# Sliding-window attention laid among its projection panels, a norm taken by columns, eight activation slots

## The reference, cut to what matters

```python
def sliding_window_sink_attention(h, w_in, sinks, w_out):
    q, k, v = split_qkv(h, w_in)          # 16 query heads, 4 key/value heads of 64
    s = jnp.einsum('bnqhgd,bnkhd->bnhgqk', qb, kw) * (HEAD_DIM_2 ** -0.5)
    s = s - slopes[:, :, None, None] * dist
    s = jnp.where(mask[None, :, None, None], s, -jnp.inf)      # this block of 128 and the one before
    m = jnp.maximum(jnp.max(s, axis=-1, keepdims=True), sink)
    p = jnp.exp(s - m)
    denom = jnp.sum(p, axis=-1, keepdims=True) + jnp.exp(sink - m)
    o = jnp.einsum('bnhgqk,bnkhd->bqnhgd', p / denom, vw)
    return o.reshape(B, T, ATTN_Q_DIM) @ w_out
```

## Time and profile before

| what | value |
|---|---|
| median of 3 runs | 2536.35 us (2536.2 to 2538.89) |
| the profiled execution's own time | 2536.2 us |
| its span | 2534.4 us |
| busy PE / DVE / ACT / POOL | 2441.7 / 1682.5 / 928.1 / 740.1 us |
| mean granted TensorE clock | 0.987 of full speed |
| matmuls | 12016 |

### The profile page before, as it was taken

The page is one execution under the profiler, slowest core; times in us unless marked ns, Lnnn a source line. Parts: engine busy times, 40 slices in busy tenths (PEclk is TensorE's granted clock), DMA queues, the critical chain, the costliest instruction groups (busy, mean ns, idle before and its releaser), DMA issues.

```text
span 2534.4 us, 35089 instructions
## 1 busy us (share of the span) xinstructions
PE 2441.7 (96%) x12016; PEld 2072.3 (82%) x12016; DVE 1682.5 (66%) x3142; ACT 928.1 (37%) x1319; POOL 740.1 (29%) x646
## 2 busy tenths in 40 slices
PE   6999999898999999999999999999999979999998
PEld 4877878686887888888888899999999756788886
DVE  4887769688566667677642478888887685444434
ACT  4223853523233333333333333333333464222222
POOL 0000000000006666676676257777641000000000
PEclk8999999999999999999999999999999999999999
DMA  6222913254234444444456689999997202222321
GB/s 257 100 73 93 350 34 129 95 190 159 100 111 139 139 148 141 150 138 149 139 171 193 206 295 366 365 366 362 360 363 258 76 25 67 91 99 91 100 99 58
DMA packets 177221, 433.59 MB, mean 171 GB/s; under 512 B 32752, under 2 KB 81904, under 8 KB 176752
## 3 DMA queue, kind: packets, MB, share of 16 engines
q1 hardware_dynamic: 123888, 331.61, 37.8%
q0 software_dynamic: 34816, 67.41, 7.7%
q10 hardware_dynamic: 18432, 33.56, 3.6%
HBM read 371.48 MB, written 61.01 MB: 171 GB/s over the span
## 4 chain that ended last, share of the span: by engine, by line
PE 87%; DVE 9%; ACT 2%; issue 1%; DMA 1%; SPq 0%; ACTq 0%; DVEq 0%
PE ps L466 17%; PE ps L467 17%; PE ps L468 17%; PE ps L802 9%; PE ps L803 9%; PE ps L801 9%; PE ps L712 2%; DVE wlo L1398 1%; DVE ar L1451 1%; PE ps L696 1%; PE ps L704 1%; PE ps L781 1%; DVE ar L1513 1%; ACT whi L936 1%; DVE rstd L1412 1%
## 5 line engine op out<-in xcount | busy, mean ns | idle before, releaser
L1398 DVE TENSOR_TENSOR wlo<-raw,whi 128x1024 fp32r<-128x1024 f32 x426 | 521.4, 1224 | 569.7 <-ACT whi L936 568.2
L2239 POOL DMA_INDIRECT w_scratch<-ar x384 | 418.8, 1091 | 953.5 <-DVE wlo L1398 854.3
L936 ACT ACTIVATE whi<-raw 128x1024 fp32r<-128x1024 f32 x424 | 448.9, 1059 | 660.0 <-PE ps L803 403.4
L466 PE MATMUL ps<-b_hi,whi 128*128 128x512 f32 x1328 | 519.6, 391 | 3.2 <-DVE wlo L1398 3.0
L468 PE MATMUL ps<-b_hi,wlo 128*128 128x512 f32 x1328 | 517.6, 390 | 0.0
L467 PE MATMUL ps<-b_lo,whi 128*128 128x512 f32 x1328 | 517.3, 390 | 0.0
L801 PE MATMUL ps<-a_hi,whi 128*128 128x384 f32 x1024 | 342.7, 335 | 0.0
L803 PE MATMUL ps<-a_hi,wlo 128*128 128x384 f32 x1024 | 342.1, 334 | 0.0
L802 PE MATMUL ps<-a_lo,whi 128*128 128x384 f32 x1024 | 342.1, 334 | 0.0
L466 PE MATMUL ps<-a_hi,whi 128*128 128x512 f32 x816 | 326.9, 401 | 8.9 <-DVE wlo L1398 7.2
L467 PE MATMUL ps<-a_lo,whi 128*128 128x512 f32 x816 | 319.6, 392 | 0.0
(11 more groups left out here) (265 smaller groups left out, 2988.7 us busy)
## 6 DMA issues: line engine op xcount, KB each, us to landing
raw<-panels SPq DMA_DIRECT2D x430, 512.0 KB, 3.4
gelu_scratch<-ar ACTq DMA_DIRECT2D x128, 256.0 KB, 2.1
w_scratch<-rstd SPq DMA_DIRECT2D x32, 768.0 KB, 10.9
ar<-w_scratch SPq DMA_DIRECT2D x128, 192.0 KB, 4.7
ar<-gelu_scratch SPq DMA_DIRECT2D x128, 192.0 KB, 5.6
...
```

The lines of the kernel that those rows point to most:

```text
L466: pe.matmul(bank, w_h, hi[:, k, :], start=(k == 0), stop=False)
L936: act.activation(whi[:, u % SPLIT, :], raw[:, u % RAW, :], ACT.Copy).then_inc(hi_ready, 1)
L1398: dve.tensor_tensor(wlo[:, u % SPLIT, :], raw[:, u % RAW, :], f32(whi[:, u % SPLIT, :]), ALU.subtract).then_inc(lo_ready, 1)
L2239: nc.gpsimd.indirect_dma_start(experts, bass.IndirectOffsetOnAxis(offs[:, k:k + 1], 0), vals[:, k:k + 1], None)\
```

## The change: what it does

- SP loads the attention's 12 panels in another order (`SW_ORDER`): key 0, value 0, queries 0 to 3, key 1, value 1, queries 4 to 7. From the seventh on all but one use bank 3 (`SWB`), and each waits until its predecessor is drained.
- The pairs go by key tile and, within it, from block 3 down to block 0. Scores, turns and value products of pairs 0 to 2 (and the scores and turns of pair 3) stand between panels 6 to 11; the rest follows. `out_half` runs the two first SO panels in halves among the last turns. The orders on PE, ACT and DVE are written out anew. SO panels use banks 4 to 7.
- One tiny DVE instruction less in `swa_bias`.
- The query norm: the sum of squares is taken as four columns (128 x 4), root and reciprocal are of 128 x 4, four matmuls spread the result into bank 5, and `norm_apply` reads it from PSUM.
- One of the folds moves from the WO panels to the CO panels (5 and 5 instead of 4 and 6), the loads and sums of their columns move with them; the sum that came after the norm comes after WO panel 6.
- Gelu's tiles use eight slots, four in `sq` and `nt`; its loop on ACT is written out.
- Semaphores of several table loads are merged.

```diff
-SWB = (0, 2, 3, 1)
+SWB = (0, 2, 3, 1, 0, 2, 3, 3, 3, 3, 3, 3)
+SW_ORDER = (0, 2, 4, 5, 6, 7, 1, 3, 8, 9, 10, 11)
...
-ge_slot = area(A_GE, 4, T)
+ge_four = area(A_GE, 4, T)
+ge_slot = [ge_four[:, s, :] for s in range(4)] + [sq[:, s, :] for s in range(2)] + [nt[:, s, :] for s in range(2)]
...
+def values_bank(m):
+    return 2 if m < 3 else 2 + m % 2
...
-    pair_at = {3: 2, 4: 3, 8: 4, 9: 5, 11: 6, 12: 7, 13: 8, 14: 9, 19: 10, 20: 11, 21: 12, 22: 13, 23: 14, 24: 15}
+    pair_at = {3: 2, 4: 3, 8: 4, 9: 5, 11: 6, 12: 7, 13: 8, 14: 9, 16: 10, 18: 11, 19: 12, 20: 13, 21: 14, 22: 15}
...
+    for n, w in enumerate(SW_ORDER):
+        sp.wait_ge(lo_ready, SW + n - RAW + 1 - U)
+        sp.dma_start(raw[:, (SW + n) % RAW, :], panels[SW + w]).then_inc(landed[(SW + n) % RAW], 16)
...
-        if k in (3, 5):
-            mod2_sums((k + 5) // 2)
-    norm_total(2, rstd[:, :])
+        if k in (1, 4, 6):
+            mod2_sums({1: 4, 4: 5, 6: 6}[k])
+    pe.wait_ge(sq_used, 3 * KT - 1)
+    for t in range(TT):
+        pe.matmul(ps[:, 4, t:t + 1], rstd[:, t * P:(t + 1) * P], ones[:, 0:1], start=(t == 0), stop=False)
+    pe.wait_ge(sq_ready, 3 * KT)
+    for t in range(TT):
+        last = pe.matmul(ps[:, 4, t:t + 1], sq[:, (KT - 1) % 2, t * P:(t + 1) * P], ones[:, 0:1], start=False, stop=(t == TT - 1))
+    last.then_inc(sq_used, 1)
+    pe.wait_ge(rstd_ready, 3)
+    for t in range(TT):
+        last = pe.matmul(ps[:, 5, t * P:(t + 1) * P], root_col[:, t:t + 1].to_broadcast([P, P]), ident, start=True, stop=True)
+    last.then_inc(root_out, 1)
     pe.wait_ge(mod_done, 4)
-    mod2_sums(6)
...
-    for u in range(4):
-        first = u == 0
-        panel(SW + u, u, ps[:, SWB[u], :], a_hi, a_lo, r_of(SW) + u + 1, (h_ready, 3 * KT) if first else None,
+    def swa_panel(p):
+        first = p == 0
+        panel(SW + p, p % 4, ps[:, SWB[p], :], a_hi, a_lo, r_of(SW) + (p + 1 if p < 7 else p + 4), (h_ready, 3 * KT) if first else None,
               (lambda k: norm_stat(3, k, bank=1)) if first else None)
-        if u == 2:
-            pe.wait_ge(rt_ready, 4)
-    for u in range(2):
+    def turn_v(u, bank):
         pe.wait_ge(v2_feat, u + 1)
         for s in range(TT):
-            last = pe.transpose(ps[:, 4 + u, s * P:(s + 1) * P], v2_feat_sb[:, u, s * P:(s + 1) * P], ident)
+            last = pe.transpose(ps[:, bank, s * P:(s + 1) * P], v2_feat_sb[:, u, s * P:(s + 1) * P], ident)
         last.then_inc(v2_turned, 1)
-    groups = [(b, kt, half) for b in range(TT) for kt in range(2) for half in range(2)]
+    groups = [(b, kt, half) for kt in range(2) for b in reversed(range(TT)) for half in range(2)]
...
+        if m == 0:
+            pe.wait_ge(v2_done, 2)
+        elif m < 3:
+            pe.wait_ge(o2, m)
+        else:
             pe.wait_ge(o2, m - 1)
+        if m == 3:
+            pe.wait_ge(bank_free, r_of(SW) + 16)
...
+    def out_half(u, half):
+        if half == 0:
+            pe.wait_ge(lo_ready, SO + u + (1 - U))
+            pe.wait_ge(bank_free, r_of(SO) + u + 1)
+            pe.wait_ge(bias2, 4 * len(groups))
+            pe.wait_ge(o2, TT)
+        else:
+            pe.wait_ge(o2, 2 * TT)
+        for k in range(4 * half, 4 * half + 4):
+            last = split3(ps[:, 4 + u, :], u, k, b_hi[:, k, :], b_lo[:, k, :], k == 0, k == KT - 1)
+        if half:
+            last.then_inc(used, 1)
+    swa_panel(0)
+    swa_panel(1)
+    swa_panel(2)
+    turn_v(0, 4)
+    pe.wait_ge(rt_ready, 4)
+    swa_panel(3)
+    swa_panel(4)
+    norm_total(4, rstd1, bank=6)
+    swa_panel(5)
+    swa_panel(6)
+    pe.wait_ge(v2_done, 1)
+    pe.wait_ge(rt_ready, 5)
+    pe.wait_ge(bank_free, r_of(SW) + 10)
+    swa_scores(0)
+    swa_panel(7)
     swa_scores(1)
-    for m in range(len(groups) // 2):
-        if m + 2 < len(groups) // 2:
-            swa_scores(m + 2)
-        swa_turn(2 * m)
-        if m:
-            swa_values(m - 1)
-        swa_turn(2 * m + 1)
-    swa_values(len(groups) // 2 - 1)
-    def last_outputs(k):
-        if k == KT // 2 - 1:
-            pe.wait_ge(o2, len(groups) // 2)
-    pe.wait_ge(o2, len(groups) // 2 - 1)
-    strips(SO, KT, b_hi, b_lo, each=last_outputs)
+    swa_panel(8)
+    swa_turn(0)
+    turn_v(1, 2)
+    swa_scores(2)
+    swa_turn(1)
+    swa_panel(9)
+    swa_values(0)
+    swa_turn(2)
+    swa_scores(3)
+    swa_turn(3)
+    swa_panel(10)
+    swa_turn(4)
+    swa_values(1)
+    swa_turn(5)
+    swa_panel(11)
+    swa_turn(6)
+    pe.wait_ge(bank_free, r_of(SW) + 16)
+    swa_scores(4)
+    swa_values(2)
+    swa_turn(7)
+    swa_scores(5)
+    swa_values(3)
+    swa_turn(8)
+    swa_scores(6)
+    swa_turn(9)
+    swa_scores(7)
+    swa_turn(10)
+    swa_values(4)
+    swa_turn(11)
+    swa_turn(12)
+    swa_values(5)
+    out_half(0, 0)
+    swa_turn(13)
+    swa_turn(14)
+    swa_values(6)
+    out_half(1, 0)
+    swa_turn(15)
+    swa_values(7)
+    out_half(0, 1)
+    out_half(1, 1)
+    for k in range(2, KT):
+        panel(SO + k, k % 4, ps[:, 4 + k % 4, :], b_hi, b_lo, r_of(SO) + k + 1)
...
-    norm_root(2, rstd[:, :])
+    act.wait_ge(sq_used, 3 * KT)
+    act.activation(root_col, ps[:, 4, 0:TT], ACT.Sqrt, bias=EPS, scale=1.0 / D).then_inc(rt_ready, 1)
...
+        n = i * 4 + u
+        if n >= 8:
+            act.wait_ge(ge_out[n % 8], n // 8 * 16)
+        act.activation(ge_slot[n % 8], ps[:, u, :], ACT.Gelu).then_inc(bank_free, 1)
         act.wait_ge(bank_free, i * 4 + (4 + r_of(EU) + u + 1))
-        act.dma_start(ge_d[bass.ds(i * 4 + u, 1)].rearrange("a p n -> (a p) n"), ge_slot[:, u, :]).then_inc(ge_out[u], 16)
+        act.dma_start(ge_d[n], ge_slot[n % 8]).then_inc(ge_out[n % 8], 16)
...
-    with act.Fori(-(-first // 4), NK // 4 - 1) as i:
-        for u in range(4):
-            gelu(i, u)
...
+    for n in range(4):
+        bias_tiles(n)
+        swa_panel_hi(6 + n)
+    bias_tiles(4)
     swa_exp(0)
     swa_exp(1)
-    for m in range(len(groups) // 2):
-        more = 2 * m + 2 < len(groups)
-        swa_out(2 * m)
-        if more:
-            swa_exp(2 * m + 2)
-        if m:
-            swa_hi(m - 1)
-        swa_out(2 * m + 1)
-        if more:
-            swa_exp(2 * m + 3)
-    swa_hi(len(groups) // 2 - 1)
+    swa_panel_hi(10)
+    swa_exp(2)
+    swa_exp(3)
+    swa_out(0)
+    swa_panel_hi(11)
+    swa_out(1)
+    swa_exp(4)
+    swa_exp(5)
+    swa_hi(0)
+    swa_out(2)
+    swa_panel_hi(12)
+    swa_out(3)
+    swa_exp(6)
+    swa_exp(7)
+    bias_tiles(5)
+    swa_out(4)
+    swa_hi(1)
+    swa_out(5)
+    bias_tiles(6)
+    bias_tiles(7)
+    swa_out(6)
+    swa_hi(2)
+    swa_out(7)
+    swa_exp(8)
+    swa_hi(3)
+    swa_exp(9)
+    swa_out(8)
+    swa_exp(10)
+    swa_out(9)
+    swa_exp(11)
+    swa_out(10)
+    swa_exp(12)
+    swa_hi(4)
+    hi_next(0, SO, 0)
+    swa_out(11)
+    swa_exp(13)
+    swa_exp(14)
+    swa_out(12)
+    swa_hi(5)
+    swa_exp(15)
+    swa_out(13)
+    swa_out(14)
+    swa_hi(6)
+    swa_out(15)
+    swa_hi(7)
...
-        if k < 4:
+        if k < 5:
...
-        if k < 6:
-            fold_half(4 + k // 2, k % 2)
+        if k < 5:
+            fold_half(4 + (k + 1) // 2, (k + 1) % 2)
...
-    norm_rstd(2)
-    norm_apply(2, x, lambda k: gs2[:, k:k + 1], lambda k: mod[:, 3 * KT + k, 0:1], b_hi, b_lo, middle=lambda: lo(WQ + 1, 1))
+    norm_rstd(2, root_col)
+    dve.wait_ge(root_out, 1)
+    norm_apply(2, x, lambda k: gs2[:, k:k + 1], lambda k: mod[:, 3 * KT + k, 0:1], b_hi, b_lo, r=ps[:, 5, :], middle=lambda: lo(WQ + 1, 1))
...
+    def key2(kt, p):
+        dve.wait_ge(used, SW + p + 1)
+        dve.tensor_tensor(k2[:, kt, :], ps[:, SWB[p], :], rstd[:, :], ALU.mult).then_inc(bank_free, 1)
+    def value2(u, p):
+        dve.wait_ge(used, SW + p + 1)
+        dve.tensor_tensor(v2_feat_sb[:, u, :], ps[:, SWB[p], :], rstd[:, :], ALU.mult).then_inc(v2_feat, 1)
+        dve.wait_ge(v2_feat, u + 1)
+        dve.sem_inc(bank_free, 1)
...
-        dve.tensor_tensor(tiny[:, o:o + 4], tiny[:, o:o + 4], col("sinks", h, 4), ALU.max).then_inc(mx2, 1)
-        dve.wait_ge(mx2, n + 1)
-        dve.tensor_scalar(tiny[:, o + 4:o + 8], tiny[:, o:o + 4], -1.0, None, ALU.mult).then_inc(nmx2, 1)
-        dve.tensor_tensor(tiny[:, o + 12:o + 16], col("sinks", h, 4), tiny[:, o:o + 4], ALU.subtract).then_inc(nmx2, 1)
+        dve.scalar_tensor_tensor(tiny[:, o + 4:o + 8], tiny[:, o:o + 4], -1.0, less_sinks[:, h:h + 4], ALU.mult, ALU.min).then_inc(nmx2, 1)
+        dve.wait_ge(nmx2, 2 * n + 1)
+        dve.tensor_tensor(tiny[:, o + 12:o + 16], col("sinks", h, 4), tiny[:, o + 4:o + 8], ALU.add).then_inc(nmx2, 1)
...
+    query2(2, 4)
+    dve.tensor_scalar(less_sinks[:, :], col("sinks", 0, NH2), -1.0, None, ALU.mult).then_inc(mx2, 1)
+    swa_panel_lo(6)
+    norm_rstd(4, rstd1)
+    query2(3, 5)
+    swa_panel_lo(7)
+    residual(0, 4)
+    key2(1, 6)
+    swa_panel_lo(8)
+    dve.wait_ge(mx2, 1)
+    dve.wait_ge(bias_ready, NH2 // 2)
+    pair_bias(0)
+    value2(1, 7)
+    swa_panel_lo(9)
+    pair_bias(1)
```

(33 more changed lines are left out.)

143 lines of the change are left out of this document (58 added, 85 removed).

## The result

The changed kernel takes **2549.1 us** in the median of 6 runs (2544.3 to 2552.9), against 2536.3 before on the same chip: ratio 1.0044, 95% interval 1.0032 to 1.0057. It is slower by 12.8 us, where 3.75 were forecast. The profiled execution took 2550.5 us, 14.3 more than the one before.

A forecast was written before the change was run, and what follows sets the result against it. Attention was taken as bound by DVE and the chain through three engines, with PE at two thirds. Stage +6.7, norm -3.4 and folds +0.45 gave +3.75 on 2536.2: 2540.0 us, range 2523 to 2548.

The forecast's parts named there:

- The stage's waits: Attention stage: PE's waits 28.1 us instead of 21.9, more among the panels and fewer behind the last, +6.2 us.
- Rival (a): Attention stage: the 9.5 us of new waits among the panels are not met and the clock stays up, 2526.0; chance 0.22.
- The stage's clock: Attention stage: lower clock behind the waits of 4.3 and 5.1 us costs 2.2 each, 4.4 against 4.7 before, -0.3 us.
- 0.8 for restarts: Attention stage: about five more panels follow an attention product, each starting with a slower first matmul, +0.8 us.
- rival (b): Attention stage: clock stays or falls low behind turns 8 and 12 (+4) and at panel 9 (+1.8), 2545.8; chance 0.25.
- nothing was slow behind a wait of 1.23: Attention stage, kernel before: full-speed work behind waits like that at 2082.66, cited against the slower-clock case.
- low spells that go on as from 2045.56: Attention stage: upper bound, 4 us more, as second scores 7 us later were slow again in the kernel before.
- The query norm: From the last x tile to the first scaled tile: 3.4 us instead of 6.8, -3.4, bounds -4.0 and -2.2.
- Reading the scale from PSUM: Query norm's scaling: costs nothing, priced at 0.74 us against 0.76; by the skill's page some 0.5 us more.
- The moved folds: CO and WO panels: CO+7 split 1.4 us late, sums behind WO+1 wait until 574.0; +0.45 us in all.
- six panels and two more sums end at 609.1: WO panels behind the sums that wait for the moved fold: PE done at 609.1, x tile 7 at 609.3.
- Gelu's slots: Expert layer's Gelu on ACT: all 128 groups waited for PE, none for a DMA, so nothing to win, 0.

The follow-up runs named there:

- the control: The changed kernel itself, measured again on another chip: 2597.0 us against 2595.2 for the kernel before, ratio 1.0011 (0.9990 to 1.0032), stage 204.3 us.
- kept_busy: Changed kernel with 14 extra unread products in each of PE's waits ahead of turns 8 and 12: 2581.6 us, ratio 1.0017 to the kernel before.
- outs_first: Changed kernel with five of ACT's copies out moved up among the panels: 2573.8 us, ratio 0.9985 to the kernel before, stage 190.5 us.
- order_norm: Kernel before with the changed attention in a further order on PE, ACT and DVE, norm by columns, eight Gelu slots, old folds: 2567.5 us, ratio 0.9874.

## Why the prediction was wrong, step by step

The forecast was 2540.0 with most of its chance within 0.2% of the old time, and the result is 2549.1: slower, outside that band and 1 us over the range. Its mechanism was right and one kind of term was mis-sized, three times: what the lower clock costs behind a wait of PE, in the attention stage, in the norm and behind the moved fold.

**The stage's waits: right.** The layout had 2.4 ahead of turn 1, 2.1 ahead of values 0 and turn 4, 1.5 and 2.1 at turns 3 and 5, then 4.3, 2.4 and 5.1. Measured were 2.94, 2.12 and 2.21, in the control 2.95, 2.12 and 2.21, then 4.3, 2.1 and 4.0; in the control and in `kept_busy`, where the clock stayed up among the panels, also those at turns 3 and 5, 1.5 and 2.0. Rival (a), that these waits would not be met, was wrong: they are met, and `outs_first` shows they came from the ACT order that the prediction named. Together they were forecast at 28.1 us and measured at 26.9 in the control and 23.6 in the first trace.

**The stage's clock: the step that failed.** The prediction took "2.2 each, 4.4, against 4.7 before: -0.3", on the ground that two waits of over 4 us have a slow stretch behind them. With its 0.8 for restarts that makes 5.2 us of clock and restarts; by the table the stage has 14.6 in its traced execution and 10.1 in the control. In the first trace 4.5 of this surplus of 9.4 came back as shorter waits, which leaves 4.9 over what was forecast. Where it was too low: the spells behind turns 8 and 12 alone cost 5.3 (`kept_busy`), a third stands behind the 2 us wait of scores 7, and among the panels the control has one more, of 1.7 us, and the first trace three, of 3.0 and twice 1.7. That last mechanism was rival (b), with 0.25; it put 5.8 us more on the stage, where 5.3 were measured, and its 2545.8 with the folds' 4.2 make 2550.0. The evidence against it, that nothing was slow behind a wait of 1.23, did not bear on waits of 2 to 3 us. The kernel before shows more, and it was not looked for. At the EU panel of 816 a wait of 2.07 was followed by a clock of 0.58. And inside the attention the second slow scores, at 2052, were read as "low spells that go on as from 2045.56"; timeline and windows show the clock up again between the two and a second fall beside a wait of only 1.42:

```profile
2052.57 0.80 PE L852 MATMUL ps<-ar 64*128 64x256 f32 x2 [1.42 <-DVE tiny L2076]
```

```profile
2049.00:2052.00 3.00, 1.37 (x10) 0.84 (x8) 2.72 (x16) 2.22 (x11) 0.00 (x0) 1.00 0.00 0
2052.00:2056.00 4.00, 3.43 (x16) 2.54 (x16) 2.88 (x13) 2.13 (x11) 0.00 (x0) 0.57 0.01 2
```

**The query norm: -3.4 forecast, -2.3 in the traced execution.** Its working holds at full clock. In the control the step from x tile 7 to the first scaled tile takes 4.24 us, and the sum gave 0.75 for the tile and 3.4. At a lower clock it takes 5.3 (changed) or 6.4 (norm alone), since eight column products take up to 1.87 us instead of 1.05, and the spreading took 2.08 where 0.9 to 1.5 was the bound. And the old form gains from a busy PE as well: with the moved folds its wide products take 1.13 instead of 2.08 and the step 6.6 instead of 7.6. So with the same folds the norm by columns is worth 1.2 (norm alone) to 1.9 us (`order_norm`) with the old ones and 1.1 to 2.4 with the moved ones, by how much of it the clock slows in the single execution, and not 3.4. Reading the scale from PSUM costs nothing: L1536 takes 0.75, as L1429 did. The Trainium skill (VectorE: DVE Perf Modes, The TRN2 errata) has a fixed 120 cycles for a source in PSUM and 58 for one in SBUF. The traces do not show that difference for an operation that reads operands from both: 0.75 us against 0.76.

**The moved folds: +0.45 forecast, +4.7 in the traced execution.** The waits are those forecast: 1.3 at the last CO panel (1.4), 1.92 ahead of the sums behind WO+1, which came at 574.26 in the execution with a full clock in CO (574.0). What is missing, 4.2 us, is mostly the clock once more. The step that failed is "six panels and two more sums end at 609.1": behind the 1.92 wait the clock fell in all seven traces with that wait (0.79 over the 8 us from 577 in the changed kernel, and over those from 574 in the control), and in none of the seven without it; the eight tiles took 2.1 us more than forecast. The fold in CO cost 1.7, forecast as 1.4. The other 1.8 us are not the folds': 0.7 that PE was late at the last GC panel already, and 1.1 for the spell that fell on CO (1.67) instead of on that panel (0.5).

**Gelu's slots: 0, right.** PE's waits in EU and EV are as before, and the kernel with the slots alone is within its noise.

**The account of the traced execution**: 3.75 forecast, +5.3 for the stage (12.0 - 6.7), +4.2 for the folds, +1.1 for the norm, -1.9 for the spell of 816 and +1.6 for that of 2178, which belong to neither kernel: 14.05, measured 14.3.
